# Self-attention's head norm in a two-layer transformer kernel: root moved into the softmax, head gains into the rotation tables, low halves moved to the vector engine

## What is computed

```python
def axial_gqa_attention(h, w_qkv, q_gain, k_gain, w_o):
    qkv = h @ w_qkv
    q = rmsnorm_2(q, q_gain)          # per head: x * rsqrt(mean(x*x) + EPS) * gain
    k = rmsnorm_2(k, k_gain)
    q = apply_axial_rope(q, cos, sin) * (HEAD_DIM ** -0.5)
    k = apply_axial_rope(k, cos, sin) # x1*c - x2*s, x2*c + x1*s
    scores = einsum(q, k)
    p = softmax(scores)
    o = einsum(p, v)
    return o @ w_o
```

## Time and profile before

| | |
|---|---|
| median of three runs | 1925.63 us |
| the profiled execution's own time | 1931.68 us |
| its span | 1929.9 us |
| TensorE matmul busy | 1830.7 us (95%) |
| TensorE weight load busy | 1626.6 us (84%) |
| VectorE (DVE) busy | 1148.2 us (59%) |
| ScalarE (ACT) busy | 943.9 us (49%) |
| GpSimd (POOL) busy | 793.0 us (41%) |
| mean granted TensorE clock | 0.983 of full speed |

### The profile page before, as it was taken

How to read it: one execution, slowest core, us unless ns; L and a number is a source line. 1 busy time by engine, 2 the same in 40 slices (tenths; PEclk the granted TensorE clock), 3 DMA queues, 4 the chain that set the end, 5 groups by cost and what they waited for, 6 DMA issues and landing times.

```text
span 1929.9 us, 32239 instructions
## 1 busy us (share of the span) xinstructions
PE 1830.7 (95%) x11558; PEld 1626.6 (84%) x11558; DVE 1148.2 (59%) x2236; ACT 943.9 (49%) x1519; POOL 793.0 (41%) x345
## 2 busy tenths in 40 slices
PE   7899989999889999999999999989999999899998
PEld 6697769889769999999999898866879987879986
DVE  5845747779764444444444445666358982458982
ACT  5466454358634444444444444545545554445543
POOL 3450147639414444444444443430324343224343
PEclk9999999999999999999999999999999999999999
DMA  6561144521245555555556655740545555325552
GB/s 262 175 216 47 56 164 155 196 99 56 95 156 187 194 176 192 181 191 180 190 184 229 227 208 181 261 158 28 174 137 175 177 187 172 116 92 177 182 184 80
DMA packets 84413, 313.27 MB, mean 162 GB/s; under 512 B 9312, under 2 KB 9440, under 8 KB 82912
## 3 DMA queue, kind: packets, MB, share of 16 engines
q1 hardware_dynamic: 82912, 304.56, 46.7%
q10 hardware_dynamic: 1408, 7.45, 1.1%
HBM read 303.58 MB, written 8.39 MB: 162 GB/s over the span
## 4 chain that ended last, share of the span: by engine, by line
issue 36%; PE 33%; DVE 16%; POOL 13%; ACT 2%; POOLq 0%; DMA 0%; DVEq 0%; ACTq 0%
PE bank L708 29%; POOL wsplit L1170 8%; DVE cv L2004 4%; DVE cv L1994 4%; POOL wsplit L1146 4%; DVE wsplit L1535 3%; PE bank L1020 2%; DVE ff L1553 1%; POOL raw L1164 1%; DVE ff L1552 1%; PE bank L850 1%; PE bank L746 0%; DVE X L1584 0%; DMA memN<-mem 0%; DVE uptmp L1759 0%
## 5 line engine op out<-in xcount | busy, mean ns | idle before, releaser
L708 PEld LDWEIGHTS bank<-HT,wsplit 128*128 128x128 f32 x5952 | 733.6, 192 | 14.7 <-issue 4.2
L708 PE MATMUL bank<-HT,wsplit 128*128 128x256 f32 x5952 | 738.3, 284 | 2.7 <-DVE HT L1569 2.7
L1170 POOL TENSOR_TENSOR wsplit<-raw,wsplit 128x1024 fp32r<-128x1024 f32 x112 | 294.6, 2630 | 389.3 <-ACT wsplit L1416 389.3
L708 PE MATMUL bank<-wsplit,wexp 128*128 128x512 f32 x1536 | 380.7, 398 | 12.7 <-DVE wexp L1912 12.7
L1146 POOL TENSOR_TENSOR wsplit<-raw,wsplit 128x1024 fp32r<-128x1024 f32 x82 | 204.9, 2498 | 403.6 <-ACT wsplit L1191 403.3
L1416 ACT ACTIVATE wsplit<-raw 128x1024 fp32r<-128x1024 f32 x238 | 251.7, 1059 | 194.9 <-PE bank L708 192.9
L708 PEld LDWEIGHTS bank<-wsplit,wexp 128*128 128x128 f32 x1536 | 282.0, 190 | 74.9 <-issue 16.6
L1892 DVE TENSOR_TENSOR wsplit<-raw,wsplit 128x1024 fp32r<-128x1024 f32 x127 | 168.6, 1327 | 243.2 <-ACT wsplit L1416 243.2
L1146 POOL TENSOR_TENSOR wsplit<-raw1b,wsplit 128x1024 fp32r<-128x1024 f32 x51 | 126.4, 2478 | 227.1 <-ACT wsplit L1191 227.1
L1191 ACT ACTIVATE wsplit<-raw 128x1024 fp32r<-128x1024 f32 x148 | 155.6, 1058 | 116.3 <-PE bank L708 108.6
L1535 DVE TENSOR_TENSOR wsplit<-raw,wsplit 128x1024 fp32r<-128x1024 f32 x66 | 98.6, 1495 | 101.1 <-ACT wsplit L1191 100.9
(11 more groups left out here) (252 smaller groups left out, 2160.1 us busy)
## 6 DMA issues: line engine op xcount, KB each, us to landing
raw<-weights SPq DMA_DIRECT2D x148, 512.0 KB, 4.0
raw<-expert_v SPq DMA_DIRECT2D x127, 512.0 KB, 3.6
raw<-expert_u SPq DMA_DIRECT2D x119, 512.0 KB, 4.5
raw1b<-weights SPq DMA_DIRECT2D x102, 512.0 KB, 4.0
raw1a<-weights SPq DMA_DIRECT2D x48, 512.0 KB, 4.3
early_u<-expert_u SPq DMA_DIRECT2D x5, 512.0 KB, 3.7
raw1a<-expert_u SPq DMA_DIRECT2D x4, 512.0 KB, 4.1
parked<-memT SPq DMA_DIRECT2D x1, 2048.0 KB, 7.4
```

The costliest lines, as they stand in the source:

```text
L708: ins = pe.matmul(out, lhsT, rhs, start=start, stop=stop, **kw)
L1170: pool.tensor_tensor(wsplit[:, s, 1, :], raw0[:, s, :], f32(wsplit[:, s, 0, :]), ALU.subtract)\
```

## The change

It does five things.

- The tables of the rotation are multiplied by the gains of the query and the key heads: eight products of 128x64 on POOL into a new tile `ropeg`, once, between the one-hot rows and the experts' low halves. DVE's multiply by the gain (line 1599) goes for query and key blocks.
- A query block is no longer divided by its root. It is rotated as it comes out of the bank (the first half of the tokens ahead of the sum of squares, the second after one low half). The inverse root of a query head goes into the attention instead: as a scale operand of the exponential on ACT, and as a product of 128x2 on DVE between the row maximum and the exponential, behind a `link`.
- A key block is still divided by its root, and then rotated with its weighted tables.
- The low halves of all units from FIRST2+8 to FIRST2+23 (the twelve of qkv and the first four of `xv1`) are made by DVE, the odd ones too, which POOL made before; POOL's loop is cut in two around them.
- ACT makes the high half of one more unit between the squares and the root of a query block.

The diff, with the declarations of the two semaphores and of the tile left out:

```diff
@@ constants
+ALONE, ALONE_END = FIRST2 + 8, FIRST2 + 24
@@ lo_made(u)
+            if u % 2 and ALONE <= u < ALONE_END:
+                return w_lo_alone, (u - ALONE) // 2 + 1
             if u % 2:
-                return w_lo_odd, u // 2 + 1
+                return w_lo_odd, u // 2 + 1 - (0 if u < ALONE else (ALONE_END - ALONE) // 2)
@@ self_jobs
+                        scale=hstat2[:, 2, :, 2 * p + i],
@@ gpsimd, after the one-hot rows
+            pool.wait_ge(in_more, 16)
+            for n in range(2):
+                gain = smalls[:, HG2][:, n * HD:(n + 1) * HD].rearrange("p (a x j) -> p a x j", a=2, x=2)
+                for w, (turned, x) in enumerate(((0, 0), (1, 1), (0, 1), (1, 0))):
+                    ins = pool.tensor_tensor(ropeg[:, n, w, :, :, :], rope2[:, turned, :, :, :],
+                                             gain[:, :, x, :].unsqueeze(1).to_broadcast([P, T, 2, 16]), ALU.mult)
+            ins.then_inc(ropeg_made, 1)
@@ gpsimd, after the experts
+            with pool.Fori(FIRST2 // RAW, ALONE // RAW) as i:
+                lo_turn(i, FIRST2, odd)
             turns = len(UNITS) // RAW
-            with pool.Fori(FIRST2 // RAW, turns) as i:
-                lo_turn(i, FIRST2, odd)
-            lo_turn(turns, FIRST2, range(1, len(UNITS) % RAW, 2))
+            with pool.Fori(ALONE_END // RAW, turns) as i:
+                lo_turn(i, ALONE_END, odd)
+            lo_turn(turns, ALONE_END, range(1, len(UNITS) % RAW, 2))
@@ scalar, head_roots: ahead is a new argument
                 act.activation(sq, hd, ACT.Square).then_inc(head_sq, 1)
+                split_to(ahead)
                 act.wait_ge(head_sum, k + 1)
@@ scalar, attention
+                            scale = -1.0 if Sb is not None else 1.0 if "scale" not in jobs[step] else jobs[step]["scale"][:, t:t + 1]
@@ scalar, the three blocks
-                head_roots(4 + n, ("qkv", n), *head_block2(n))
+                head_roots(4 + n, ("qkv", n), *head_block2(n), units_to(("qkv", n, 1)) + (4 if n < 2 else 3))
@@ vector, split_to
-                    if u % 2 == 0:
+                    if u % 2 == 0 or ALONE <= u < ALONE_END:
@@ vector, in place of rope_axial
+            def rotate_axial(hv, t, heads, kind, squared):
+                h2 = hv[:, t, heads, :].rearrange("p h (a x j) -> p h a x j", a=2, x=2)
+                x1, x2 = h2[:, :, :, 0, :], h2[:, :, :, 1, :]
+                n = heads.stop - heads.start
+                c1, s2, c2, s1 = (ropeg[:, kind, w, t, :, :].unsqueeze(1).to_broadcast([P, n, 2, 16]) for w in range(4))
+                tmp = [rtmp2[:, t, w, 0:n] for w in range(4)]
+                dve.tensor_tensor(tmp[0], x1, c1, ALU.mult)
+                dve.tensor_tensor(tmp[1], x2, s2, ALU.mult)
+                dve.tensor_tensor(tmp[2], x2, c2, ALU.mult)
+                link(dve.tensor_tensor(tmp[3], x1, s1, ALU.mult))
+                dve.wait_ge(head_sq, squared)
+                dve.tensor_tensor(x1, tmp[0], tmp[1], ALU.subtract)
+                return dve.tensor_tensor(x2, tmp[2], tmp[3], ALU.add)
+            def head_sums(k, n, sq, st):
+                dve.wait_ge(head_sq, k + 1)
+                dve.tensor_reduce(st[0], sq.rearrange("p t (h d) -> p t h d", d=HD), AXX, ALU.add).then_inc(head_sum, 1)
+            def query_block(n):
+                hd, sq, st = head_block2(n)
+                hv = hd.rearrange("p t (h d) -> p t h d", d=HD)
+                ahead = units_to(("qkv", n, 0))
+                for t in range(T):
+                    wait_freed(dve, ("qkv", n, t))
+                    if t == 0:
+                        rotate_axial(hv, 0, slice(0, 8), 0, 4 + n + 1)
+                head_sums(4 + n, n, sq, st)
+                split_to(ahead + 4)
+                link(rotate_axial(hv, 1, slice(0, 8), 0, 4 + n + 1))
+                split_to(ahead + 5)
+                dve.wait_ge(head_root, 4 + n + 1)
+                link(dve.reciprocal(st[2], st[1]))
+                dve.sem_inc(head_done, 1)
+            def key_block(n):
+                hd, sq, st = head_block2(n)
+                hv = hd.rearrange("p t (h d) -> p t h d", d=HD)
+                for t in range(T):
+                    wait_freed(dve, ("qkv", n, t))
+                head_sums(4 + n, n, sq, st)
+                dve.wait_ge(head_root, 4 + n + 1)
+                link(dve.reciprocal(st[2], st[1]))
+                link(dve.tensor_tensor(hv, hv, st[2].unsqueeze(3).to_broadcast([P, T, N_KV, HD]), ALU.mult))
+                for t in range(T):
+                    ins = rotate_axial(hv, t, slice(0, N_KV), 1, 4 + n + 1)
+                ins.then_inc(head_done, 1)
@@ vector, attention
+                            if "scale" in jobs[step]:
+                                link(ins)
+                                ins = dve.tensor_tensor(less, less, jobs[step]["scale"], ALU.mult)
```

More of the change, by code:

```diff
@@ L178, in block_stack @@
         root_table = sb("root_table", [P, 1])
+        ropeg = sb("ropeg", [P, 2, 4, T, 2, 16])
         act_e = sb("act_e", [P, 2, S])
@@ L372, in block_stack @@
         w_hi, w_freed = sem("w_hi_made"), sem("w_freed")
+        w_lo_alone, ropeg_made = sem("w_lo_odd_by_vector"), sem("rope_gains_made")
         w_lo_even, w_lo_odd, w_lo_choice = sem("w_lo_by_vector"), sem("w_lo_by_pool"), sem("w_lo_even_by_pool")
@@ L1241, in copy_keys, with head_roots @@
                 act.activation(dst[HD:P, 1:4:2, :], src[HD:P], ACT.Copy).then_inc(bank_freed["a"], 1)
-            def head_roots(k, group, hd, sq, st):
+            def head_roots(k, group, hd, sq, st, ahead=0):
                 for t in range(T):
@@ L1263, in attention @@
                             src = Sb[:, j % 2, t, 0:w] if Sb is not None else PS[j % 2][:, t * S:(t + 1) * S]
+                            scale = -1.0 if Sb is not None else 1.0 if "scale" not in jobs[step] else jobs[step]["scale"][:, t:t + 1]
                             ins = act.activation(Pb[:, j % 3, t, 0:w], src, ACT.Exp, bias=att[:, 0, j % 4, t:t + 1],
-                                                 scale=1.0 if Sb is None else -1.0, accum_out=att[:, 1, j % 4, t:t + 1])
+                                                 scale=scale, accum_out=att[:, 1, j % 4, t:t + 1])
                         ins.then_inc(s_exp, 1)
@@ L1531, in split_to @@
                 for u in range(split[0], min(u1, limit[0])):
-                    if u % 2 == 0:
+                    if u % 2 == 0 or ALONE <= u < ALONE_END:
                         dve.wait_ge(w_hi, u + 1)
                         dve.tensor_tensor(wsplit[:, u % NSPLIT, 1, :], sb_raw(u), f32(wsplit[:, u % NSPLIT, 0, :]),
-                                          ALU.subtract).then_inc(w_lo_even, 1)
+                                          ALU.subtract).then_inc(lo_made(u)[0], 1)
                     split[0] = u + 1
@@ L1617, in rope_first @@
                        [rtmp1[:, w, :, 0:n, :] for w in range(4)]).then_inc(head_done, 1)
-            def rope_axial(hv, n):
-                for t in range(T):
-                    h2 = hv[:, t, :, :].rearrange("p h (a x j) -> p h a x j", a=2, x=2)
-                    c, s = (rope2[:, w, t, :, :].unsqueeze(1).to_broadcast([P, n, 2, 16]) for w in range(2))
-                    ins = rotate(h2[:, :, :, 0, :], h2[:, :, :, 1, :], c, s, [rtmp2[:, t, w, 0:n] for w in range(4)])
+            def rotate_axial(hv, t, heads, kind, squared):
[11 more added lines that the diff above has]
+                return dve.tensor_tensor(x2, tmp[2], tmp[3], ALU.add)
@@ L1939, in _ @@
             norm_out("attn", HT)
-            hg = smalls[:, HG2].rearrange("p (n d) -> p n d", n=2)
+            dve.wait_ge(ropeg_made, 1)
             for n in range(3):
                 copy_bank(("qkv", n, 0), qkv[:, 0, 512 * n:512 * (n + 1)], bank(("qkv", n, 0))[:, :])
-                head_norm(4 + n, *head_block2(n), [(8, hg[:, 0, :])] if n < 2 else [(N_KV, hg[:, 1, :])], rope_axial,
-                          units_to(("qkv", n, 0)))
+                if n < 2:
+                    query_block(n)
+                else:
+                    key_block(n)
             split_to(units_to(("xv", 1)) + 2)
```

## The result

The changed kernel takes 1915.64 us, median of five runs (1914.66 to 1920.25), against 1927.66 us for the kernel before on the same chip (1925.39 to 1929.05). The ratio estimated from all these runs is 0.9946, 95% interval 0.9934 to 0.9957, which is 10.4 us less (8.3 to 12.7); the two medians by themselves differ by 12.0 us. Its profiled execution took 1920.25 us (span 1918.5), that of before 1931.68 us (span 1929.9). The forecast was 1915.4 us in 1912.5 to 1921.0.

A forecast was written before the change was run, and what follows sets the result against it. The prediction took TensorE (95% busy) as bounding, held up in qkv and xv1 by DVE standing beside POOL. Stage 11.8 less attention 1.2 and tables 0.4 gave 10.2 us saved: 1925.6 to 1915.4 us, range 1912.5 to 1921.

The forecast's parts named there:

- What bounds: In qkv and xv1, DVE falls behind TensorE, standing still until POOL's instructions end, about 4.2 us per block.
- The stage, 11.8 us: TensorE's qkv and xv1 matmuls run through without waits or slow clock: 12.1 us less 0.3, so 11.8 us saved.
- The walk of the block: DVE's instructions in a query block, checked in order against deadlines: 11.1 us against TensorE's 10.98, no deadline missed.
- the 0.3 us booked for xv1 unit 4 beside POOL: In the key block, DVE's low half of that unit may stand for POOL's next one, ending slightly late: 0.3 us lost.
- Self-attention, 1.2 us lost: DVE's added product and ACT's longer exponential show only while the attention's pipeline fills (0.8 us) and drains (0.4 us).
- Tables, 0.4 us lost: POOL's eight products before the experts take 0.4 us each, 3.2 us against 2.8 free, so DVE stands still once.
- Rivals B and C: Table products on POOL at their upper end, 1922.8 us, chance 0.06; or over 1.7 us each, slower, 1931.4 us, chance 0.04.
- Sum: Whole kernel: 11.8 - 1.2 - 0.4 = 10.2 us saved, from a median of 1925.6 to 1915.4 us.
- Rival A: In the stage, low halves cost DVE as much as they free; 4.1 us saved in all, 1921.5 us, chance 0.16.
- Rival D: Something else than DVE's lateness makes the waits; the stage keeps 67 us, 1.6 us slower, 1927.2 us, chance 0.04.

The follow-up runs named there:

- low halves alone: Kernel before, with VectorE making all low halves of qkv units 0 to 11 and xv1 units 0 to 3, ScalarE's high halves ahead of the root: 1919.06 us, ratio 0.9958.
- the longer range: Changed kernel with VectorE's range of low halves extended by 8 units, to the end of xv1: 1914.31 us, ratio 0.9932.
- the order alone: Changed kernel with the rotation of a query block's first half put back behind the sum of squares: 1920.68 us, ratio 0.9975.
- The run without the additions: Changed kernel without the attention's product with the queries' root and without the exponential's scale: one run, 1914.48 us.
- the first run: Not labelled in the text; presumably the changed kernel as first measured against the kernel before: 1915.64 us, ratio 0.9946.
- the run with POOL beside VectorE: Changed kernel with POOL also subtracting 1024 columns of constants into scratch eight times in the stage: one run, 1931.83 us.

## Why the prediction was right, and where it was not

**What bounds.** The reading of the earlier trace rows, that DVE stands still beside POOL until POOL's instruction ends, is shown three ways: the rows fall to 1.2 us when POOL goes (low halves alone, VectorE's work larger), the long rows come back when POOL subtracts constants beside DVE (12.4 us in the stage), and a 128x128 multiply stands as long as a 128x1024 one. In the first of these the high halves ahead of the root were moved as well; what they are worth by themselves was not run.

**The stage, 11.8 us.** It gave 11.46. The walk of the block (11.1 us, measured 11.19) held, and the 0.3 us booked for xv1 unit 4 beside POOL is the 0.35 us that the longer range gives back. The 0.34 us that are missing lie in TensorE's own pace: all 240 matmuls were reckoned at that of qkv's first 96, 21.97 us, and xv1's 96 take 22.56 without a wait. What the text had but never priced is the order. It spoke of two multiplies and of standing; the walk put the first rotation into the wait for the square without a number for it. Taking away any one part costs nearly the same: low halves 4.6 us (60.05), all changes of the norm, the order among them, 5.3 (60.72), the order alone 5.3 (60.74). In each of the three DVE is late enough for POOL to meet it in the key block, once or twice.

**Self-attention, 1.2 us lost.** The size is right (1.14 us measured), the period stayed 2.50 us and the exponential takes 0.56 us. The step that failed is that nothing was booked on the other side: before, the first scores ran partly at 1.2 GHz (granted clock 0.66 over 1300 to 1305), in the changed profile at 1.00. That returned about 0.9 us, so that the trace shows +0.26 and not +1.14. It is no certain gain: the run without the additions had the same stage as the change and yet an intermediate clock there. What sets the clock there, beyond the waits in the stage, stays open.

**Tables, 0.4 us lost.** Nothing was lost. The product takes 0.29 us, below the 0.4 I took, and fits into the 2.8 us. The estimate from the Trainium skill's GPSIMD Engine Reference (Elementwise, side-by-side cycle accounting), 0.43 us, was too high as well. The step behind the 0.4 us, that DVE would stand still while POOL makes its products, is wrong for products this short: 32 of them put 0.18 us on the path. Rivals B and C fell with their condition, a product of 1.3 us or more. What products that long would cost was not run; POOL's subtractions of 2.4 us do hold DVE up.

**Sum.** -11.46 and +0.26 are 11.2 us saved, where 10.2 was forecast: two costs were booked too high (0.9 and 0.4 us), the stage's gain by 0.3. That 1915.4 and the measured 1915.64 us agree to 0.2 us is in part luck: the forecast was taken from 1925.63, the median of three runs, and the five have 1927.66, 2.0 us more; the medians' difference of 12.0 us lies above the 10.2 by nearly as much. Within the interval of 8.3 to 12.7 us no finer agreement is shown.

**Rival A** said that the low halves cost DVE as much as they free. That is refuted: the move, with ACT's high halves made earlier and the norm as before, took the block from 17.1 to 14.7 us. The rule of the Trainium skill in Perfetto Trace Analysis (Optimizing Scalar/DVE Operations), that moving work between GPSIMD and DVE might not help, does not hold here in the direction from GPSIMD to DVE, because a subtraction costs DVE 1.2 us itself and up to 2.2 us when POOL has it. What the Trainium skill says in SBUF — State Buffer (Who interferes with whom), that the port is held for a whole instruction, agrees with these runs: DVE's rows end 0.1 to 1.1 us behind POOL's, never before them. Rival D fell with the first run.

## What to carry to other kernels

When an engine's row takes two or three times its usual duration, look for what the other engine was doing at that moment and compare the ends: here a POOL instruction of 2.4 us cost DVE up to 2.2 us, more than the 1.2 us for which DVE does the same work itself. Fill the waits in an engine's own chain (a square, a high half) with work that doesn't depend on it before looking for work to remove. And undo parts one at a time: near saturation, taking away any of three parts cost about 5 us of 11, because a little lateness brings on the next collision.

## What the runs showed of the hardware

- The cost of a meeting depends on what is left of POOL's instruction, not on DVE's: 2.50 us for a 128x128 multiply that takes 0.28, 2.62 us for one of 128x256 that takes 0.41. DVE's sum over 128x1024 with one input ran beside POOL at its normal 1.21 us.
- POOL stands for DVE as well. In the run with POOL beside VectorE two of its subtractions start 0.04 and 0.05 us behind a low half of DVE and take 3.44 us; the low half takes its usual 1.23. The other six take 2.40 to 2.53.

```profile
1230.01 1.23 DVE L1560 TENSOR_TENSOR wsplit<-raw1b,wsplit 128x1024 fp32r<-128x1024 f32 x1 [1.08 <-ACT wsplit L1213]
1230.05 3.44 POOL L1191 TENSOR_TENSOR qkT<-smalls 128x1024 f32<-128x1024 f32 x1 [3.76 <-ACT wsplit L1213]
```

- POOL's products of 128x64 took 0.29 us alone and 0.37 us on average beside DVE; four of them beside a DVE subtraction lengthened it by 0.1 to 0.2 us.
- The first eight scores behind the stage took 1.99 us at a granted clock of 1.00, and 3.5 to 3.8 us in the five experiments that had a wait of over 1 us in the stage; with a stage like the change's they also took 2.72 us once.
